# TensorE's order within a step of two attentions: value products ahead of the next pair's transposes

## The chip, the cores and the metric

The kernel is one program on one core of a Trainium2 chip. The metric is the time of one execution on the device in microseconds (us), of which the median of three runs is given. TensorE multiplies matrices, VectorE (DVE in the profile) and ScalarE (ACT) work on elements and may read TensorE's output banks, GpSimd (POOL) works on elements outside those banks, SyncE (SP) issues most transfers.

## The reference, cut to what matters

Two transformer layers and a third hybrid block are computed for 512 tokens and 16 meta tokens ahead of them. The change touches the attentions of the first two layers. Layer 0 has a differential attention of 4 heads (two softmaxes each, one subtracted from the other) and a dense attention of 8 heads over 2 key heads; layer 1 has 16 heads over 2 key heads that see a window of 128 tokens to each side, the meta tokens, and a sink.

```python
def _diff_attention(q, k, v, lam, table, pos):
...
        s = jnp.einsum('bqhcd,bshcd->bhcqs', qb, k).astype(jnp.float32) * scale + bias[None, :, None]
        p = jax.nn.softmax(s, axis=-1)
        attn = p[:, :, 0] - lam * p[:, :, 1]
        return jnp.einsum('bhqs,bshv->bqhv', attn.astype(v.dtype), v)
...
def _gqa_dense(q, k, v):
...
        s = jnp.einsum('bqkgd,bskd->bkgqs', qb, k).astype(jnp.float32) * scale
        p = jax.nn.softmax(s, axis=-1)
        return jnp.einsum('bkgqs,bskd->bqkgd', p.astype(v.dtype), v)
...
def _window_gqa(q, k, v, sinks, table):
...
        s = jnp.einsum('bqkgd,bskd->bkgqs', qb, kc).astype(jnp.float32) * scale + bias[None]
        s = jnp.where(visible, s, NEG_INF)
        sink_col = jnp.broadcast_to(sink[None, :, :, None, None], s.shape[:-1] + (1,))
        p = jax.nn.softmax(jnp.concatenate([s, sink_col], axis=-1), axis=-1)[..., :-1]
        return jnp.einsum('bkgqs,bskd->bqkgd', p.astype(vc.dtype), vc)
```

## The kernel before, in words

Every engine has its own instruction stream, written by hand, and the streams meet at semaphores. Most of the program is projections: TensorE multiplies weights, held as a high and a low part (`w_hi`, `w_lo`), with activations held likewise, three products for one (lines 1032 to 1034).

Between the projections lie two calls of `attend`: one for layer 0 (34 pairs, which the text calls A for the 17 of the differential attention and B for the 17 of the dense one), one for layer 1 (32 pairs, called C). A **pair** is a block of 128 queries with two heads (or two softmaxes). One pair takes four pieces of work on TensorE and three elsewhere:

- `scores(s)` (L1120): queries times keys of both heads into the banks `acc`. It waits for `s_stored`, by which DVE tells that it has taken the scores of the pair before.
- DVE's `tops(s)` (L2416) adds the bias, finds the row maximum and writes `probs`; ACT's `exponentials` (L1755) run once for each head; DVE's `shares(s)` (L2427 and L2430, or L2433 to L2435) and POOL (L923) divide by the sums. They tell `probs` and `scaled`.
- `turn(s)` (L1140 to L1148), four steps after its scores (`LAG = 4`): TensorE transposes the probabilities into the two banks `tps`, and the 16 meta columns into a bank of `ops_`. In part of the B pairs it also transposes one or two finished blocks of A that are carried along (L1148). It waits for `probs`, for `scaled`, for `p_stored` of the pair before (its `tps` banks must have been copied out), and for `o_stored` of its `ops_` bank, of which there are two that alternate.
- ACT's `copies(s)` (L1764, L1766, L1773) takes meta columns, carried blocks and the transposed probabilities out to `probsT`, and tells `p_stored`. In ACT's order it stands between the exponentials of head 0 and of head 1 of a later pair. It waits for `p_full`, which the last transpose of `turn(s)` tells.
- `values(s)` (L1162 in A, L1168 in B and C): transposed probabilities times values, into the same `ops_` bank. It waits for `p_stored` of this pair.
- DVE's `outputs(s)` (L2444 in A; L2449, L2451, L2453 in B and C) takes the result out and tells `o_stored`.

The steps are a loop over `s` on each engine. Step `s` on TensorE holds `turn(s - 4)`, `values(s - 5)` and `scores(s)`. In the first four steps pieces of a projection (`fill`) stand ahead of the scores. In the five steps behind the last scores, pieces of the next projection (`drain`, L960 to L962) take their place; the last two pieces in layer 0 wait for a result of `outputs`. `tps` has no second copy: its two banks are one for each head.

Of the kernel before, what the change touches and what calls it, by code (L numbers as in the profile page):

```python
# [53 lines left out]
LAG = 4  # L54
# [150 lines left out]
def transposed_blocks_program(nc, a, out):  # L205
# [80 lines left out]
    with ctx:  # L286
# [369 lines left out]
        for i in range(8):  # L656
            for t in range(4):
# [3 lines left out]
                n = (hi - lo) * P  # L661
# [274 lines left out]
        def _(pe):  # L936
# [9 lines left out]
            def close(ins, b, kind=""):  # L946
                ins.then_inc(sems[f"{kind}full{b}"], T.up(f"{kind}full{b}"))
                T.saw(f"{kind}stored{b}")
# [146 lines left out]
            def attend(pairs, metaT, fill, drain):  # L1095

                n = len(pairs)
# [3 lines left out]
                def scores(s):  # L1101
                    p = pairs[s]
                    if s and pairs[s - 1].differ and not p.differ:
                        T.saw("kswap_in", 5 * 16)
                        pe.wait_ge(sems["kswap_in"], T.at("kswap_in"))
                        T.saw("vmeta_in", 32)
                        pe.wait_ge(sems["vmeta_in"], T.at("vmeta_in"))
                    free = 2 * s if p.wide else 2 * s - 2
                    if s == 0:
                        for kind in ("stored0", "stored1"):  # L1110
                            pe.wait_ge(sems[kind], T.at(kind))
                    if free > 0:
                        pe.wait_ge(sems["s_stored"], stored_0 + free)
                    if p is A_METAS:
                        T.saw("q_metas", 2)
                        pe.wait_ge(sems["q_metas"], T.at("q_metas"))
                    left = [sum(x[0] == o for x in p.products) for o in range(2)]
                    for o, rows, c, w, q, keys, first, last in p.products:
                        bank = flat[o][:, LEAD:] if p.wide else acc[s % 2][:, o, :]
                        ins = mm(bank[rows, c:c + w], q, keys, start=first, stop=last)  # L1120
                        left[o] -= 1
                        if not left[o]:
                            ins.then_inc(sems[f"s_full{o}"], T.up(f"s_full{o}"))

                def turn(s):
                    p = pairs[s]
                    if s == 0:
                        for kind in ("t_stored0", "t_stored1"):
                            pe.wait_ge(sems[kind], T.at(kind))
                    pe.wait_ge(sems["probs"], probs_0 + s + 1)  # L1130
                    if not p.differ:
                        pe.wait_ge(sems["scaled"], scaled_0 + p.scaled)
                    if s:
                        pe.wait_ge(sems["p_stored"], copied_0 + s)
                    p.b = open_("o_")
                    unit = ident[0:p.nq, 0:p.nq]
                    _, which, to = p.turned_metas(ops_[p.b])
                    if p.joint:
                        both_heads = probs_1[0:p.nq, s % RING].rearrange("p o n -> p (o n)")
                        nc.tensor.transpose(to[:, 0, :], both_heads[:, SEQ:SEQ + 2 * N_META], unit)  # L1140
                    for o in (1,) if p.differ else (0, 1):
                        S = probs_1[0:p.nq, s % RING, o, :]
                        if not p.joint:
                            nc.tensor.transpose(to[:, o - which.start, :], S[:, p.meta:p.meta + N_META], unit)  # L1144
                        for k, c in enumerate(p.tiles[o]):
                            ins = nc.tensor.transpose(tps[o][:, k * P:k * P + p.nq], S[:, c:c + P], unit)  # L1146
                    for a, to in p.carried(ops_[p.b]):
                        ins = nc.tensor.transpose(to, a.dest, ident[:])  # L1148
                    ins.then_inc(sems["p_full"], T.up("p_full"))

                def values(s):
                    p = pairs[s]
                    pe.wait_ge(sems["p_stored"], copied_0 + s + 1)
                    b, last = p.b, len(p.tiles[0])

                    def weights(o, k):
                        return probsT_1[:, s % 2, o, k, :] if k < last else metaT[:, s % 2, 0 if p.joint else o, :]

                    if p.differ:
                        for k in range(last + 1):  # L1160
                            for rows, v in p.v:
                                ins = mm(ops_[b][rows, 0:v[k].shape[1]], weights(1, k)[:, rows], v[k],  # L1162
                                         start=k == 0, stop=k == last)
                    else:
                        for sums in (p.sums_of[n:n + 2] for n in range(0, len(p.sums_of), 2)):
                            for k in range(last + 1):
                                for o, rows, queries, to in sums:
                                    ins = mm(ops_[b][rows, to], p.v[o][k], weights(o, k)[:, queries],  # L1168
                                             start=k == 0, stop=k == last)
                    close(ins, b, "o_")  # L1170

                for s in range(n + LAG + 1):
                    if 0 <= s - LAG < n:
                        turn(s - LAG)
                    if 0 <= s - LAG - 1 < n:
                        values(s - LAG - 1)
                    if s < len(fill):
                        fill[s]()
                    if s < n:
                        scores(s)  # L1180
                    if s == n:
                        pe.wait_ge(sems["s_stored"], stored_0 + 2 * n)
                    if s >= n:
                        drain[s - n]()
# [128 lines left out]
            def value_tokens(qkv, v):  # L1313
# [10 lines left out]
                     [(1, k) for k in (0, 1, 2)]]  # L1324
            begun, drain = unit_ahead(MIX["even_out"], early, (3, 4))
            attend(A_PAIRS + B_PAIRS, metaT_e, unit_in_parts(LEN), drain)
            for kind in ("o_stored0", "o_stored1"):
                pe.wait_ge(sems[kind], T.at(kind))
# [14 lines left out]
            pe.wait_ge(sems["kswap_in"], T.at("kswap_in"))  # L1343
            begun, drain = unit_ahead(MIX["odd_out"], [[(0, k)] for k in range(LAG + 1)], ())
            attend(C_PAIRS, metaT_o, unit_in_parts(SEQ), drain)
            for kind in ("o_stored0", "o_stored1"):
                pe.wait_ge(sems[kind], T.at(kind))
# [2066 lines left out]
```

## Time and profile before

| | |
|---|---|
| median of 3 runs | 2178.78 us (2178.54 to 2185.92) |
| the profiled execution, first to last instruction | 2178.0 us; no other time of its own is shown |
| TensorE busy | 2152.0 us, 99% |
| VectorE, ScalarE, GpSimd busy | 1094.7, 817.1, 877.4 us |
| mean granted clock of TensorE | 0.996 |
| bytes moved | 210.69 MB |

The three runs lie within 0.34%, two of them within 0.01%. The profiled execution is 0.5 to 0.8 us shorter than the two fast ones, as its span leaves out what lies ahead of the first and behind the last instruction.

### The profile page before, as it was taken

The numbers are of one execution on the slowest core, as the hardware profiler recorded it, in microseconds if no ns is written. First come the engines' busy times: TensorE is split into PE (matmuls) and PEld (weight loads), VectorE is DVE, ScalarE is ACT, GpSimd is POOL, SyncE is SP. The second block draws the span as 40 slices with busy tenths as digits, with TensorE's granted clock in tenths as the row PEclk, the third lists the DMA queues.
The fourth block names the chain that finished last, engine by engine and source line by source line (L and its number), as shares of the span: only waits on it lengthen the run. The fifth ranks groups of instructions, "written<-read, shape, count | busy, mean of one in ns | idle before, by whom it ended". The sixth has DMA issues, their size and how long they took to land.

```text
span 2178.0 us, 32989 instructions
## 1 busy us (share of the span) xinstructions
PE 2152.0 (99%) x13003; PEld 1826.1 (84%) x13003; DVE 1094.7 (50%) x1677; ACT 817.1 (38%) x1358; POOL 877.4 (40%) x396
## 2 busy tenths in 40 slices
PE   8999999999999999999999999999999999999998
PEld 7987899999999767788888778888878788888886
DVE  5577655623633375430243379555664554443225
ACT  4248544213333374431243323243423432322224
POOL 2323534433443454444444433333434344444442
PEclk9999999999999999999999999999999999999999
DMA  5720145333433602333333375233223243332331
GB/s 161 173 57 2 37 129 157 88 88 117 127 96 91 188 2 59 88 96 97 88 95 97 87 166 168 64 92 87 79 80 94 78 117 95 96 94 84 96 102 61
DMA packets 375111, 210.69 MB, mean 97 GB/s; under 512 B 26464, under 2 KB 367553, under 8 KB 374097
## 3 DMA queue, kind: packets, MB, share of 16 engines
q1 hardware_dynamic: 364726, 192.60, 31.2%
q10 hardware_dynamic: 10266, 16.41, 2.8%
q8 instruction: 87, 1.43, 0.3%
q14 instruction: 32, 0.25, 0.0%
HBM read 196.96 MB, written 15.40 MB: 98 GB/s over the span
## 4 chain that ended last, share of the span: by engine, by line
issue 42%; PE 35%; POOL 19%; DVE 2%; ACT 1%; POOLq 0%; DVEq 0%; ACTq 0%
POOL w_lo L894 19%; PE acc L1032 8%; PE acc L1033 8%; PE acc L1034 8%; PE ops L1168 2%; PE acc L1120 2%; PE tps L1146 2%; PE ops L1162 1%; PE ops L1144 1%; PE acc L960 1%; PE tps L1092 0%; PE acc L962 0%; PE acc L961 0%; DVE probs L2416 0%; DVE a_n L2568 0%
## 5 line engine op out<-in xcount | busy, mean ns | idle before, releaser
L894 POOL TENSOR_TENSOR w_lo<-raw,w_hi 128x1024 fp32r<-128x1024 f32 x326 | 793.5, 2434 | 1165.7 <-ACT w_hi L1624 1155.9
L1624 ACT ACTIVATE w_hi<-raw 128x1024 fp32r<-128x1024 f32 x325 | 344.4, 1060 | 1028.8 <-PE acc L1034 1004.7
L1032 PE MATMUL acc<-hr_hi,w_hi 128*128 128x512 f32 x1056 | 421.8, 399 | 0.6 <-DVE qkv L3030 0.6
L1034 PE MATMUL acc<-hr_hi,w_lo 128*128 128x512 f32 x1056 | 417.8, 396 | 0.0
L1033 PE MATMUL acc<-hr_lo,w_hi 128*128 128x512 f32 x1056 | 417.6, 395 | 0.0
L1032 PE MATMUL acc<-hn_hi,w_hi 128*128 128x264 f32 (+1 forms) x872 | 256.9, 295 | 2.7 <-DVE hn_lo L2500 1.5
L1033 PE MATMUL acc<-hn_lo,w_hi 128*128 128x264 f32 (+1 forms) x872 | 253.4, 291 | 0.0
L1034 PE MATMUL acc<-hn_hi,w_lo 128*128 128x264 f32 (+1 forms) x872 | 253.2, 290 | 0.0
L1032 PEld LDWEIGHTS acc<-hr_hi,w_hi 128*128 128x128 f32 x1056 | 198.4, 188 | 49.4 <-issue 1.8
L1034 PEld LDWEIGHTS acc<-hr_hi,w_lo 128*128 128x128 f32 x1056 | 198.4, 188 | 48.0
L1033 PEld LDWEIGHTS acc<-hr_lo,w_hi 128*128 128x128 f32 x1056 | 198.5, 188 | 47.4 <-issue 0.7
L1032 PEld LDWEIGHTS acc<-hn_hi,w_hi 128*128 128x128 f32 x872 | 164.2, 188 | 7.1 <-DVE hn_lo L2500 1.4
L1033 PEld LDWEIGHTS acc<-hn_lo,w_hi 128*128 128x128 f32 x872 | 164.2, 188 | 2.6
L1034 PEld LDWEIGHTS acc<-hn_hi,w_lo 128*128 128x128 f32 x872 | 163.5, 188 | 2.4
L1032 PE MATMUL acc<-mid_hi,w_hi 128*128 128x264 f32 x512 | 146.7, 286 | 0.3 <-DVE hid L2879 0.3
L1033 PE MATMUL acc<-mid_lo,w_hi 128*128 128x264 f32 x512 | 146.1, 285 | 0.0
L1034 PE MATMUL acc<-mid_hi,w_lo 128*128 128x264 f32 x512 | 145.9, 285 | 0.0
L923 POOL TENSOR_SCALAR probs<-probs,stat 128x528 f32<-128x528 f32 (+2 forms) x49 | 73.6, 1502 | 108.2 <-DVE stat L2427 108.0
L1755 ACT ACTIVATE probs<-probs,stat 128x528 f32<-128x528 f32 (+2 forms) x132 | 85.8, 650 | 44.9 <-DVE stat L2416 44.9
L1032 PE MATMUL acc<-mr_hi,w_hi 128*128 128x512 f32 x256 | 101.3, 396 | 0.0
L1034 PE MATMUL acc<-mr_hi,w_lo 128*128 128x512 f32 x256 | 101.3, 396 | 0.0
L1033 PE MATMUL acc<-mr_lo,w_hi 128*128 128x512 f32 x256 | 101.3, 396 | 0.0
(467 smaller groups left out, 3788.3 us busy)
## 6 DMA issues: line engine op xcount, KB each, us to landing
raw<-in_w_up SPq DMA_DIRECT2D x64, 512.0 KB, 4.0
raw<-in_w_down SPq DMA_DIRECT2D x64, 512.0 KB, 3.7
raw<-in_w_in SPq DMA_DIRECT2D x56, 512.0 KB, 3.8
raw<-in_w_ffn_gate SPq DMA_DIRECT2D x22, 512.0 KB, 3.8
raw<-in_w_ffn_up SPq DMA_DIRECT2D x22, 512.0 KB, 3.8
raw<-in_w_in_even SPq DMA_DIRECT2D x18, 512.0 KB, 8.6
raw<-in_w_ffn_down SPq DMA_DIRECT2D x16, 512.0 KB, 3.7
raw<-in_w_in_odd SPq DMA_DIRECT2D x10, 512.0 KB, 5.6
```

The costliest lines, as they stand in the source:

```text
L894: nc.gpsimd.tensor_tensor(w_lo[:, part], raw[:, slot], w_hi[:, part].bitcast(F32), ALU.subtract).then_inc(sems["lo"], T.up("lo"))
L923: nc.gpsimd.tensor_scalar(S, S, st[:, 4:5], None, ALU.mult).then_inc(sems["scaled"], T.up("scaled"))
L960: mm(out, w_hi[:, part, k, :], x_hi, start=first, stop=False)
L1032: mm(out, w_hi[:, part, w0 + k, :], xh, start=s0, stop=False)
L1033: mm(out, w_hi[:, part, w0 + k, :], xl, start=False, stop=False)
L1034: ins = mm(out, w_lo[:, part, w0 + k, :], xh, start=False, stop=s1)
L1120: ins = mm(bank[rows, c:c + w], q, keys, start=first, stop=last)
L1144: nc.tensor.transpose(to[:, o - which.start, :], S[:, p.meta:p.meta + N_META], unit)
L1146: ins = nc.tensor.transpose(tps[o][:, k * P:k * P + p.nq], S[:, c:c + P], unit)
L1168: ins = mm(ops_[b][rows, to], p.v[o][k], weights(o, k)[:, queries], start=k == 0, stop=k == last)
L1624: fn(w_hi[:, n % 2], raw[:, n % 4], ACT.Copy).then_inc(sems["hi"], T.up("hi"))
L1755: fn(S, S, ACT.Exp, bias=st[:, o:o + 1], scale=-1.0, accum_out=p.den(st, o)).then_inc(sems["exp"], T.up("exp"))
```

## The change

The two calls in TensorE's step change places. Nothing else is changed: both wait for the same semaphores at the same values, and no other engine's stream differs.

```diff
                 for s in range(n + LAG + 1):
+                    if 0 <= s - LAG - 1 < n:
+                        values(s - LAG - 1)
                     if 0 <= s - LAG < n:
                         turn(s - LAG)
-                    if 0 <= s - LAG - 1 < n:
-                        values(s - LAG - 1)
                     if s < len(fill):
                         fill[s]()
                     if s < n:
                         scores(s)
```

TensorE in the attention of layer 1 before the change, from the scores of a pair with 273 keys on (`acc` holds scores, `tps` and `ops` receive transposes, `probsT` are the copied ones, `vtok` the values; in brackets the semaphores that an instruction waits for):

```order
L1120 MATMUL acc<-keys_o,qkv_o 128x273 [waits s_stored]
L1120 MATMUL acc<-keys_o,qkv_o 128x273
L1144 MATMUL ops<-ident,probs 16x128 [waits p_stored,o_stored0,scaled,probs]
L1146 MATMUL tps<-ident,probs 128x128 x3
L1144 MATMUL ops<-ident,probs 16x128
L1146 MATMUL tps<-ident,probs 128x128 x3
L1168 MATMUL ops<-probsT,vtok_o 64x128 [waits p_stored]
L1168 MATMUL ops<-probsT,vtok_o 64x128 x3
L1168 MATMUL ops<-metaT_o,vtok_o 64x128 x2
L1120 MATMUL acc<-keys_o,qkv_o 128x401 [waits s_stored]
```

The same place in the changed kernel:

```order
L1120 MATMUL acc<-keys_o,qkv_o 128x273 [waits s_stored]
L1120 MATMUL acc<-keys_o,qkv_o 128x273
L1168 MATMUL ops<-probsT,vtok_o 64x128 [waits p_stored]
L1168 MATMUL ops<-probsT,vtok_o 64x128 x3
L1168 MATMUL ops<-metaT_o,vtok_o 64x128 x2
L1144 MATMUL ops<-ident,probs 16x128 [waits p_stored,o_stored0,scaled,probs]
L1146 MATMUL tps<-ident,probs 128x128 x3
L1144 MATMUL ops<-ident,probs 16x128
L1146 MATMUL tps<-ident,probs 128x128 x3
L1120 MATMUL acc<-keys_o,qkv_o 128x401 [waits s_stored]
```

Between a pair's transposes (L1144, L1146) and its own value products (L1168), the value products of the pair before and the scores stood before; now the scores alone stand there.

ACT in the same attention, which is the same in both kernels:

```order
L1764 ACTIVATE metaT_o<-ops 16x256 [waits p_full]
L1773 ACTIVATE probsT<-tps 128x2x256
L1755 ACTIVATE probs,stat<-probs,stat 128x273 [waits s_stored] x2
L1764 ACTIVATE metaT_o<-ops 16x256 [waits p_full]
L1773 ACTIVATE probsT<-tps 128x2x384
```

The copies of one pair stand between the exponentials of two heads; nothing moved here.

TensorE behind the scores in layer 0, where pieces of the next projection (L960) stand in their place, as a difference:

```order
+L1168 MATMUL ops<-probsT,vtok_e 64x128 x8
+L1168 MATMUL ops<-metaT_e,vm_e 64x128 x2
 L1140 MATMUL ops<-ident,probs 32x128
 L1146 MATMUL tps<-ident,probs 128x128 x8
 L1148 MATMUL ops<-ident,qkv_e 128x128
-L1168 MATMUL ops<-probsT,vtok_e 64x128 x8
-L1168 MATMUL ops<-metaT_e,vm_e 64x128 x2
 L960 MATMUL acc<-mix_e_hi,w_hi 128x264
 L961 MATMUL acc<-mix_e_lo,w_hi 128x264
```

Here too the value products of the pair before have moved ahead of the transposes (L1140, L1146, L1148), and the projection's products follow these directly.

## Rows read from the trace of the kernel before

**Rows 1.** The page's first part: busy time, share of the span and instructions.
```profile
PE 2152.0 (99%) x13003; PEld 1826.1 (84%) x13003; DVE 1094.7 (50%) x1677; ACT 817.1 (38%) x1358; POOL 877.4 (40%) x396
```

**Rows 2.** Busy time, granted clock and transfers in A, B and C (stretches named in the text).
```profile
core 0: us, PE busy (x) PEld busy (x) DVE busy (x) ACT busy (x) POOL busy (x), PEclk, DMA share, GB/s
143.37:192.37 49.00, 48.30 (x405) 38.10 (x403) 41.68 (x129) 39.12 (x125) 3.04 (x2) 1.00 0.01 1
192.37:257.65 65.28, 61.38 (x674) 49.83 (x672) 42.27 (x138) 49.49 (x119) 38.25 (x34) 1.00 0.01 2
755.47:837.90 82.43, 80.48 (x774) 54.62 (x774) 57.94 (x231) 62.69 (x177) 38.91 (x30) 1.00 0.01 1
```

**Rows 3.** Timeline, TensorE in C: start us, us, what, [idle before <-releaser].
```profile
786.41 0.73 PE L1120 MATMUL acc<-keys_o,qkv_o 64*128 64x273 f32 x4
787.29 0.27 PE L1144 MATMUL ops<-ident,probs 128*16 128x128 f32 x1 [0.15 <-DVE mix_o_lo L2453]
789.06 0.94 PE L1120 MATMUL acc<-keys_o,qkv_o 64*128 64x401 f32 x4
...
789.94 0.27 PE L1144 MATMUL ops<-ident,probs 128*16 128x128 f32 x1
```

**Rows 4.** Timeline, DVE in C: the last instruction of an output.
```profile
786.85 0.29 DVE L2453 TENSOR_TENSOR mix_o_lo<-ops,mix_o_hi 128x128 fp32r<-128x128 f32 x1
```

**Rows 5.** Timeline, end of C: value products begin, ACT copies the transposes just finished.
```profile
833.72 0.78 ACT L1773 ACTIVATE probsT<-tps 128x768 f32<-128x768 f32 x1
...
835.98 0.88 PE L1168 MATMUL ops<-probsT,vtok_o 128*64 128x128 f32 x12
836.09 0.37 ACT L1764 ACTIVATE metaT_o<-ops 16x256 f32<-16x256 f32 x1 [1.59 <-PE tps L1146]
836.37 0.57 ACT L1773 ACTIVATE probsT<-tps 128x512 f32<-128x512 f32 x1
```

**Rows 6.** Timeline, B: two copies of ACT around its table loads, TensorE's next transposes.
```profile
204.36 1.00 ACT L1773 ACTIVATE probsT<-tps 128x1024 f32<-128x1024 f32 x1
...
209.90 1.00 ACT L1773 ACTIVATE probsT<-tps 128x1024 f32<-128x1024 f32 x1
...
211.15 0.27 PE L1140 MATMUL ops<-ident,probs 128*32 128x128 f32 x1 [1.73 <-ACT probsT L1773]
```

**Rows 7.** Timeline, TensorE in a step of B with nothing carried.
```profile
199.09 0.28 PE L1140 MATMUL ops<-ident,probs 128*32 128x128 f32 x1
...
201.42 0.49 PE L1120 MATMUL acc<-qkv_e 64*128 64x264 f32 x1
...
202.51 0.29 PE L1140 MATMUL ops<-ident,probs 128*32 128x128 f32 x1
```

**Rows 8.** Timeline, B with two carried blocks: TensorE, ACT's copies, the end of the output.
```profile
228.02 1.09 PE L1168 MATMUL ops<-probsT,vtok_e 128*64 128x128 f32 x16
...
228.12 0.27 ACT L1764 ACTIVATE metaT_e<-ops 32x128 f32<-32x128 f32 x1 [0.58 <-PE ops L1148]
...
228.80 1.00 ACT L1773 ACTIVATE probsT<-tps 128x1024 f32<-128x1024 f32 x1
...
229.26 1.16 PE L1120 MATMUL acc<-kx_e,qkv_e 64*128 64x264 f32 x8
...
230.23 0.28 DVE L2453 TENSOR_TENSOR mix_e_lo<-ops,mix_e_hi 128x128 fp32r<-128x128 f32 x1
...
230.66 0.27 PE L1140 MATMUL ops<-ident,probs 128*32 128x128 f32 x1 [0.24 <-DVE mix_e_lo L2453]
```

**Rows 9.** Timeline, end of B: a piece of the projection, the next transposes.
```profile
245.04 0.39 PE L960 MATMUL acc<-mix_e_hi,w_hi 128*128 128x264 f32 x1
...
246.24 0.27 PE L1140 MATMUL ops<-ident,probs 128*32 128x128 f32 x1
```

**Rows 10.** Timeline, A: ACT's copies of a pair.
```profile
156.72 0.25 ACT L1764 ACTIVATE metaT_e<-ops 16x128 f32<-16x128 f32 x1
156.87 0.57 ACT L1773 ACTIVATE probsT<-tps 128x512 f32<-128x512 f32 x1
```

**Rows 11.** The one stretch of 5 us with a low granted clock (columns as rows 2).
```profile
460.00:465.00 5.00, 5.00 (x54) 5.00 (x52) 0.04 (x1) 0.00 (x0) 0.00 (x0) 0.52 0.36 108
```

## The prediction

> **What bounds the kernel now.** I read the page first, then the busy time by stretches, then the timeline of the attentions. The page says that TensorE is busy 99% of the span [rows 1], so each microsecond that it waits more ends up in the time, unless something later takes it back. By stretches [rows 2] the attentions are where it waits: A is 49.0 us with 0.7 idle, B 65.3 with 3.9, C 82.4 with 1.95. The clock is full in all three, and DMA stands still (share 0.01), so the change can act only through TensorE's own order and its partners ACT and DVE. The timeline then tells for whom it waits. In C the transposes that follow the scores of 273 keys start at 787.29, though these scores end at 787.14; DVE's output ended at 786.85 + 0.29 = 787.14 as well, and its word takes 0.15 us more [rows 3, 4]. In B with two carried blocks the output ends at 230.51, and the transposes start at 230.66 after 0.24 idle [rows 8]. So today a turn waits for the output of the pair two before it, which has only the scores' time to be taken out. That is what the change relieves: with the value products first, the output has the time of a whole turn more.
>
> **What the change takes instead.** Call the times of the pieces V (values), T (turn), S (scores). ACT's copies of a pair must come between its T and its V. Before, V of the pair before and S lay in between; now S alone does. The copies need a time L from the end of T to the start of V:
>
> - ACT starts 0.10 to 0.11 after the next piece of TensorE has begun (835.98 to 836.09 [rows 5], 228.02 to 228.12 [rows 8]).
> - The meta columns hold it 0.28 in C (836.09 to 836.37 [rows 5]), 0.15 in A [rows 10]; for B I take 0.17, between the two. In B two carried blocks lengthen 228.12 to 228.80 = 0.68 [rows 8], so each carried block is (0.68 - 0.17) / 2 = 0.25.
> - The large copy is 0.57 for two key tiles and 0.78 for three in C [rows 5], 1.00 in B [rows 6, 8], 0.57 in A [rows 10].
> - From the end of ACT's copy to TensorE's start: 209.90 + 1.00 = 210.90 to 211.15, that is 0.25, of which 0.03 is the weight load that goes ahead, so 0.22 [rows 6]. The nearest other row, DVE to TensorE, has 0.15 [rows 4].
>
> So L is 0.11 + 0.28 + 0.57 + 0.22 = 1.18 in C with two tiles and 1.39 with three; in B 0.11 + 0.17 + 1.00 + 0.22 = 1.50, 1.75 and 2.00 with 0, 1 and 2 carried blocks; in A 0.11 + 0.15 + 0.57 + 0.22 = 1.05.
>
> The cover S is, start to start, 1.09 in A and B (201.42 to 202.51 [rows 7]), 0.88 in C with 401 keys (789.06 to 789.94 [rows 3]), and for 273 keys 0.73 - 0.06 = 0.67, since the record of 401 is 0.94 for the 0.88. Tiles and keys go together, as the scores four pairs on are those of the same query block. Where the scores are over, a piece of the projection covers: 1.20 in B [rows 9]; in C I take 0.88, its three products of 512 columns being near to the scores of 401 keys.
>
> ACT is free when T ends. The exponential that stands ahead of the copies comes behind DVE's read of one head's scores, and I estimate both done 1.5 us after these end; V and T lie between, 1.77 us in C (787.29 to 789.06 [rows 3]) and 3.42 - 1.09 = 2.33 in B [rows 7]. Behind the waiting V stand T and S on TensorE's queue, and for S waits DVE. Both then move as one, and no other queue holds anything of this. The SP and POOL queues are not passed by anything.
>
> **The sum, C.** Each of 27 turns that scores follow waits L - S = 1.18 - 0.67 or 1.39 - 0.88, that is 0.51 both times: 13.8 us. The four last ones wait 0.30, 0.51, 0.51, 0.30: 1.6. Turn 0 waits for its copies before and after alike. What goes is today's waiting: 1.95 us idle [rows 2], and in 13 steps another 0.07 which the record's tail hides (787.29 - 786.41 - 0.67 = 0.21 in place of the 0.15 shown): 2.9. **C: 15.4 - 2.9 = +12.5 us.**
>
> **B.** Five turns with nothing carried wait 1.50 - 1.09 = 0.41: 2.05. One meets ACT's table loads: its copies end 5.54 us after those before it (204.36 to 209.90 [rows 6]) where a step is 3.42 (199.09 to 202.51 [rows 7]): 2.12, in place of today's 1.73. One with one carried block waits 0.66. Four with two wait 0.91 each, 3.64; a fifth is followed by the meta queries' scores, 12 products for 4 on half the rows, which I estimate at twice 1.09, so it waits for nothing. The turn of the meta queries copies its meta columns as C does and one block: 0.77. Four at the end wait 0.80, 0.53, 0.53 and, where only 3 of 9 products are left for cover (0.40), 1.35. Sum 12.4. What goes: 3.9 idle [rows 2] and 7 times 0.07: 4.4. **B: +8.0 us.**
>
> **A.** L = 1.05 against S = 1.09: nothing waits, but with 0.04 us to spare. The idle 0.7 us [rows 2] goes. **A: -0.7 us.**
>
> Nothing takes this back later: behind both attentions TensorE runs projections whose weights ACT and POOL prepare after the copies, and the prepared unit has about 0.3 us to spare by my count. The sum is 12.5 + 8.0 - 0.7 = **+19.8 us on the profiled 2178.0: 2197.8**. The median of the runs is 0.8 above the profiled span, so the forecast is **2198.5 us** (+0.9%).
>
> **Bounds.** The least sure term is ACT's word to TensorE, paid in 47 waits. By DVE's 0.15 instead of 0.22 to 0.25 it is 3.3 to 4.7 us less. From above, 0.1 us more each time, for a start of TensorE out of a stop, makes 4.7 us more, and 17 times 0.1 in A, whose spare is thin, 1.7: 2194 to 2205.
>
> **The rivals.**
>
> *The output wait is the dearer one (not slower).* The two orders trade one wait for another. If ACT's copies came back within 0.67, 0.88 and 1.09 us, all waits for outputs would go, 0.7 in A, 4.4 - 1.73 = 2.7 in B and 2.9 in C, 6.3 us in all: 2172.5. It decides at L = S. The rows put L of C 0.51 above it with both parts recorded, so I give it 0.04, of which 0.01 for a gain above 0.5%.
>
> *Half is hidden.* If TensorE's waits in a step also let DVE and ACT get ahead, so that every second copy comes early, about 10 us remain: 2188.8. Against it: the copies hang on the end of T by `p_full`, and cannot begin before it. 0.05.
>
> *ACT becomes the bound.* Copies that wait longer push the second head's exponentials and all behind them. ACT is 80% used in A and 76% in B and C [rows 2]. If each of 66 steps took 0.3 us more on top, it would be 2218. In steps longer than today's there is more room for ACT, not less. 0.02.
>
> *The clock.* In the one stretch with a low clock TensorE shows no idle time at all; it runs the small products of `kernel_products` there, and has fallen to about 0.52, near the lower level of 1.2 GHz [rows 11]. So waiting is not the only thing that lowers it, and the 1.73 us of idle time in B left the clock of its stretch at 1.00 [rows 2, 6]. If it fell to 1.2 GHz for all of C, C's 80.5 us of work would double: 2279. 0.02. The Trainium skill (TensorE: Matmul & The Clock Gate, section "A second HAM failure mode: psum-queue depth-cycling") speaks against this change: short idle times between groups of products, as each step cycles through the banks, can make the clock swing between its levels. By it C and perhaps B would go this way; here no row shows it so far, as waits of 0.15 to 0.24 us in many steps left the clock full.
>
> *The change doesn't do what it says* is ruled out by the order of the instructions: every step is turned round, and only on TensorE.
>
> **How the numbers follow.** The forecast has 0.87. 0.5% is 10.9 us, about what a measurement of this kernel can tell from no change. Slower by more: 0.87 + 0.02 + 0.02 = 0.91; within: 0.03 + 0.05 = 0.08; faster: 0.01. The range takes the bounds 2194 to 2205, goes down to 2190 for part of the hidden case, and up to 2206 for the scatter of runs: 2190 to 2206.
>
> **What would show it.** In the profile after, the first value product of nearly every step (L1168) has idle time ahead of it released by ACT's L1773, some 0.4 to 0.5 us in C, 0.3 to 0.9 in B, and in A (L1162) none or hundredths. The transposes (L1140, L1144) no longer wait for DVE. Four steps of C take 4 x 0.51 - 2 x 0.21 = 1.6 us more than today, C's stretch is 95 us long and B's 73. The rest of the program keeps its length. I am wrong if the waits at L1168 are there but the stretches don't grow, if A's value products wait 0.2 us or more, or if the clock of a stretch falls.

## The result, and the profile after

The changed kernel takes **2193.97 us** (median of 5 runs, 2193.05 to 2194.66). The kernel before, run beside it, takes 2180.6 (5 runs, 2178.54 to 2185.92). The ratio is 1.0057, interval 1.0041 to 1.0073: slower by 0.6%. The forecast was 2198.5 in 2190 to 2206, so direction and range held, and the size was 4.5 us too large. The profiled execution has a span of 2192.7 us against 2178.0, which is 14.7 us more where the sum said 19.8.

The page's first part after, to be held against [rows 1]:

```profile
PE 2155.4 (98%) x13003; PEld 1827.5 (83%) x13003; DVE 1090.9 (50%) x1677; ACT 819.6 (37%) x1358; POOL 876.5 (40%) x396
```

The same stretches of A, B and C as in [rows 2], each from the like instruction to the like instruction, with the same columns:

```profile
143.30:192.42 49.12, 49.12 (x404) 38.35 (x402) 41.59 (x129) 40.68 (x125) 3.12 (x2) 1.00 0.00 1
192.42:263.04 70.62, 61.54 (x674) 49.57 (x672) 41.36 (x138) 48.92 (x119) 37.95 (x33) 1.00 0.01 2
762.34:852.37 90.03, 81.14 (x774) 54.17 (x774) 55.42 (x232) 62.68 (x177) 39.16 (x30) 1.00 0.01 1
```

A is 49.12 us long (before 49.00), B 70.62 (65.28), C 90.03 (82.43). TensorE's busy time grows by only 0.8, 0.2 and 0.7 us in them; B now has 9.1 us idle and C 8.9. The clock is full in all three, as it was. What TensorE waits for is one thing (waits of TensorE in C, then in B; columns: who waits and for whom, us in total, times, longest):

```profile
PE ops L1168 <- ACT probsT L1773: 9.2, 32, 0.5
```

```profile
PE ops L1168 <- ACT probsT L1773: 9.1, 16, 2.0
```

The value products of all 32 pairs of C and of 16 of the 17 of B wait for ACT's copy, and in B and C no row of the transposes names DVE any more: the wait of [rows 3] and of [rows 8] is gone. Now two steps of C on TensorE:

```profile
790.48 0.94 PE L1120 MATMUL acc<-keys_o,qkv_o 64*128 64x401 f32 x4
791.70 0.88 PE L1168 MATMUL ops<-probsT,vtok_o 128*64 128x128 f32 x12 [0.28 <-ACT probsT L1773]
...
793.48 0.73 PE L1120 MATMUL acc<-keys_o,qkv_o 64*128 64x273 f32 x4
794.49 0.33 PE L1168 MATMUL ops<-probsT,vtok_o 128*64 128x128 f32 x2 [0.28 <-ACT probsT L1773]
```

and ACT in the same two:

```profile
790.59 0.37 ACT L1764 ACTIVATE metaT_o<-ops 16x256 f32<-16x256 f32 x1 [0.90 <-PE tps L1146]
790.87 0.78 ACT L1773 ACTIVATE probsT<-tps 128x768 f32<-128x768 f32 x1
...
793.59 0.37 ACT L1764 ACTIVATE metaT_o<-ops 16x256 f32<-16x256 f32 x1 [0.68 <-PE tps L1146]
793.87 0.57 ACT L1773 ACTIVATE probsT<-tps 128x512 f32<-128x512 f32 x1
```

The terms of the forecast stand here one behind the other. ACT starts 0.11 after the scores have begun, spends 0.28 until the large copy begins, and 0.78 or 0.57 on it: all four are as forecast. But the copy ends at 791.65, and the value products start at 791.70. **ACT's word, the time from the end of its copy to TensorE's start, takes 0.05 us, not 0.22.** So the lag is 1.22 and 1.01 against covers of 0.88 and 0.67, and a step waits 0.34, where 0.51 stood in the sum. (The record shows 0.28, since the scores' record has a tail of 0.06.) It is 0.05 in B as well, at the shortest wait (202.32 + 1.00 = 203.32, and the products at 203.37) and at the longest, 2.05 us, where ACT loads its tables (its copy ends at 212.52):

```profile
202.32 1.00 ACT L1773 ACTIVATE probsT<-tps 128x1024 f32<-128x1024 f32 x1
```

```profile
203.37 1.09 PE L1168 MATMUL ops<-probsT,vtok_e 128*64 128x128 f32 x16 [0.17 <-ACT probsT L1773]
...
212.57 1.09 PE L1168 MATMUL ops<-probsT,vtok_e 128*64 128x128 f32 x16 [2.05 <-ACT probsT L1773]
```

### The profile page after: what moved, and what is told of

It is laid out like the page before. It is cut to its first block, busy times and chain, and to the rows that moved or that the text cites. A ratio compares the mean times of both kernels' runs of the same rounds, so it can differ in the third digit from the quotient of the medians.

```text
span 2192.7 us, 32989 instructions
## 1 busy us (share of the span) xinstructions
PE 2155.4 (98%) x13003; PEld 1827.5 (83%) x13003; DVE 1090.9 (50%) x1677; ACT 819.6 (37%) x1358; POOL 876.5 (40%) x396
## 3 DMA queue, kind: packets, MB, share of 16 engines
q1 hardware_dynamic: 364726, 192.60, 31.1%
## 4 chain that ended last, share of the span: by engine, by line
issue 42%; PE 35%; POOL 19%; ACT 3%; DVE 2%; POOLq 0%; DVEq 0%; ACTq 0%
POOL w_lo L894 19%; PE acc L1032 8%; PE acc L1033 8%; PE acc L1034 8%; PE ops L1168 2%; PE tps L1146 2%; ACT probsT L1773 2%; PE acc L1120 1%; PE ops L1162 1%; PE ops L1144 1%; ACT metaT_o L1764 1%; PE tps L1092 0%; PE acc L960 0%; PE acc L962 0%; PE acc L961 0%
## 5 line engine op out<-in xcount | busy, mean ns | idle before, releaser
L1032 PEld LDWEIGHTS acc<-mid_hi,w_hi 128*128 128x128 f32 x512 | 97.4, 190 | 0.5 <-DVE hid L2879 0.5
```

Source lines behind the costliest of these rows:

```text
L1032: mm(out, w_hi[:, part, w0 + k, :], xh, start=s0, stop=False)
```

## The experiments

A trace is easiest to compare in five stretches of TensorE. "Lead" goes to the first scores of layer 0. "A+B" goes from there to the end of that attention's last value product, and "C" is the like in layer 1. "Between" lies between the two attentions, and "rest" behind C. One profile of each kernel, us:

| kernel | lead | A+B | between | C | rest | span |
|---|---|---|---|---|---|---|
| before | 131.06 | 127.90 | 486.46 | 93.36 | 1339.22 | 2178.0 |
| after | 130.99 | 133.36 | 488.14 | 100.76 | 1339.45 | 2192.7 |
| e1 new order in C alone | 129.49 | 127.90 | 486.30 | 100.76 | 1343.25 | 2187.7 |
| e2 new order in A and B alone | 130.85 | 134.76 | 486.36 | 93.33 | 1346.70 | 2192.0 |
| e3 bank wait late | 130.98 | 126.53 | 484.67 | 91.79 | 1340.13 | 2174.1 |
| e4 two copies | 130.22 | 129.41 | 486.62 | 92.49 | 1342.06 | 2180.8 |
| e5 copy wait last | 130.80 | 128.33 | 486.42 | 96.49 | 1346.76 | 2188.8 |
| e6 three more waits | 131.34 | 133.39 | 486.38 | 100.78 | 1339.01 | 2190.9 |
| e7 values last | 129.39 | 159.02 | 488.23 | 114.12 | 1339.44 | 2230.2 |
| e8 before, rot_s first | 131.09 | 127.92 | 486.26 | 93.36 | 1339.67 | 2178.3 |
| e9 after, rot_s first | 129.25 | 133.37 | 485.23 | 100.75 | 1340.90 | 2189.5 |
| e10 bank wait late, rot_s first | 131.42 | 126.55 | 488.58 | 91.76 | 1340.49 | 2178.8 |
| e11 copy wait last, rot_s first | 131.02 | 128.30 | 486.25 | 96.53 | 1340.10 | 2182.2 |
| e12 one more wait | 131.30 | 133.39 | 486.39 | 100.78 | 1342.84 | 2194.7 |

Kernels with like code in an attention agree there to 0.05 us, except where the clock fell (e2, e4, below). The change itself is therefore 5.46 + 7.40 = **12.9 us**. The other 1.8 of the 14.7 lie in stretches that the change does not touch, and those differ by up to 7.8 us ("rest" in e5 and e6) between kernels with the same code there.

**e1 and e2: one attention at a time.** The step's order hangs on a condition, which in e2 is turned round (e1 against the changed kernel):

```diff
+                    first = not pairs[0].wide
-                    if 0 <= s - LAG - 1 < n:
+                    if first and 0 <= s - LAG - 1 < n:
                         values(s - LAG - 1)
                     if 0 <= s - LAG < n:
                         turn(s - LAG)
+                    if not first and 0 <= s - LAG - 1 < n:
+                        values(s - LAG - 1)
```

> New order in the attention of layer 1 alone, old order in layer 0. The theory (the copies' lag L against the scores' time S, step by step) says that each attention pays for itself: C was 7.4 us longer in the changed kernel, so the span is 2178.0 + 7.4 = 2185.4 us, with waits for ACT's copies (L1773) only in C, 0.34 us a step. The second theory, that 1.8 us of the loss came from the small products of kernel_products falling differently against the clock, says that these take 9.2 us here as before, since they come ahead of C. The rival, that the loss hangs on something shared by both attentions or carried from one to the other, has no reason for 7.4.

> New order in layer 0 alone. The theory: A unchanged within 0.2 us, B +5.3, C as before. With the clock's part, the small products begin 5.4 us later as in the changed kernel and take 10.9 us instead of 9.2: span 2185.1. If the clock's part is chance from run to run and not set by where the products begin, the span is 2183.3 or anything up to 2 us around it. With the run of layer 1 alone the two gains should add up to the 14.7 us of the whole change.

Measured: e1 2187.82 us (8 runs, 2185.44 to 2194.61), ratio 1.0034, interval 1.0021 to 1.0048. e2 2191.52 (7 runs, 2181.64 to 2193.95), ratio 1.0037, interval 1.0022 to 1.0052. The kernel before had 2179.9 beside them (30 runs, 2176.51 to 2187.36). The stretches give what was expected: e1 carries all of C and nothing of A and B, e2 the reverse and 1.4 us more. Against the median of the kernel before, e1 is 7.9 us slower (7.4 expected) and e2 11.6 (5.3 to 7.1 expected); the interval of e2's ratio, 4.8 to 11.3 us, is wide enough to hold what was expected. The profiled execution of e2, 14.0 us longer than that of the kernel before, shows two places for the excess. The first is behind ACT's table loads in B, where TensorE's wait of 2.05 us was followed in this run by a lower clock (windows of e2, columns as [rows 2]):

```profile
205.00:210.00 5.00, 4.83 (x51) 3.75 (x49) 3.61 (x13) 4.29 (x7) 1.62 (x1) 1.00 0.02 3
210.00:215.00 5.00, 2.95 (x31) 2.40 (x28) 2.63 (x9) 3.80 (x9) 0.90 (x2) 0.88 0.00 0
215.00:220.00 5.00, 5.00 (x44) 3.68 (x42) 2.24 (x8) 2.72 (x6) 5.00 (x6) 0.78 0.00 2
```

The same place with the same wait kept the full clock in after, e6, e9 and e12, and fell to 0.66 in e4. The fall costs e2 134.76 - 133.36 = 1.4 us. The second place, in "rest", is met again in e5.

**e3: the output wait without the new order.** The gain that the change was after, in the old order. A turn first transposes into `tps`, which needs no `ops_` bank, and waits for the bank only ahead of the meta columns:

```diff
-                    p.b = open_("o_")
                     unit = ident[0:p.nq, 0:p.nq]
+                    heads = (1,) if p.differ else (0, 1)
+                    for o in heads:
+                        for k, c in enumerate(p.tiles[o]):
+                            nc.tensor.transpose(tps[o][:, k * P:k * P + p.nq], probs_1[0:p.nq, s % RING, o, c:c + P], unit)
+                    p.b = open_("o_")
...
```

> Old order of the steps; inside a turn the probabilities are transposed first and only then does TensorE wait for the output bank (o_stored), ahead of the meta columns. The theory says that the old order waits for outputs only as these have the scores' time alone; they get 0.44 to 0.87 us more, so these waits vanish: 2.9 us in C, about 1.7 in B (the wait of the next projection at its end stays), up to 0.7 in A: 4.6 to 5.3 us less, span about 2173, give or take 1.8 for the clock of the small products. If TensorE's waits there were not for the bank but the cost of going from one kind of product to another, nothing changes, or it becomes slower by the extra waits.

Measured: span 2174.1; A+B is 1.4 and C 1.6 us shorter, 2.9 together where 4.6 to 5.3 were expected. TensorE's idle time did fall by 1.8 us in A+B and 2.1 in C, but its busy time grew by 0.5 in each, which the expectation had at nothing. TensorE and DVE in C of e3:

```profile
780.35 0.73 PE L1120 MATMUL acc<-keys_o,qkv_o 64*128 64x273 f32 x4
...
780.80 0.29 DVE L2454 TENSOR_TENSOR mix_o_lo<-ops,mix_o_hi 128x128 fp32r<-128x128 f32 x1
781.02 0.65 PE L1139 MATMUL tps<-ident,probs 128*128 128x128 f32 x4
```

The turn starts 0.67 behind the scores and 0.07 before DVE's output has ended: the cover of 0.67 for 273 keys, which the forecast had only estimated, is right. The median did not show the gain: 2181.98 (12 runs, 2176.07 to 2189.5), ratio 1.0009, interval 0.9998 to 1.002. They scatter over 13 us; e8 to e10 deal with that.

**e4: shorter copies in the new order.** TensorE tells ACT by a new semaphore `p_half` when the transposes of head 0 are done, and ACT copies these while head 1 is transposed:

```diff
+                        if o == 0:
+                            ins.then_inc(sems["p_half"], T.up("p_half"))
...
+                    if not p.differ:
+                        act.wait_ge(sems["p_half"], half_0 + 1 + sum(not x.differ for x in pairs[:s]))
+                        fn(probsT_1[:, s % 2, 0, 0:k, 0:p.nq].rearrange("p k q -> p (k q)"),
+                           both[:, 0, 0:k * P], ACT.Copy).then_inc(sems["metas"], T.up("metas"))
                     act.wait_ge(sems["p_full"], full_0 + s + 1)
```

> Changed kernel, but ACT copies head 0's transposes as soon as they are done, then the meta columns and head 1. L falls to 0.80 and 0.90 us in C (waits 0.13 and 0.02 a step instead of 0.34), in B to 0.90, 1.15 and 1.40 (waits 0, 0.06, 0.31 instead of 0.24, 0.49, 0.74). The theory: C 8.3 us shorter and B 5.1, so the span goes from 2192.7 to 2179.3, give or take 1.8. The rival, that ACT is the bound in the new order, says that two copies in place of one (0.15 us more of ACT in each step) make it slower: 2192.7 + 49 x 0.15 = 2200.

Measured: 2181.25 us (10 runs, 2177.1 to 2188.19), ratio 1.0009, interval 0.9995 to 1.0022. C is 92.49, 8.3 us less than after, as expected: the wait was the copies' length, and with half of it ahead of the turn's end it is nearly gone (0.3 us left at L1170 in C). A+B is 129.41, 4.0 less than after where 5.1 was expected, in a run whose clock was 0.66 from 210 to 215 us. The rival of ACT as the bound, which had the span at 2200, falls.

**e5: which wait stands last.** In a turn of the old order, the wait for `p_stored` is put behind the one for `o_stored`:

```diff
-                    if s:
-                        pe.wait_ge(sems["p_stored"], copied_0 + s)
                     p.b = open_("o_")
+                    if s:
+                        pe.wait_ge(sems["p_stored"], copied_0 + s)
```

> Old order; in a turn the wait for ACT's copies (p_stored) stands behind the wait for the output bank instead of ahead of it, with the same values. My sum had 0.22 to 0.25 us from the end of ACT's copy to TensorE's transposes, measured where another wait stood behind it; in the changed kernel the value products, with this as their only wait, start 0.05 us after the copy. If a wait that stands behind the released one costs time, the one place in B where transposes wait for ACT (the table loads) shows less than 0.25 us here, about 0.15, and the waits for DVE's outputs 0.05 to 0.1 us more than 0.15. If it is the kind of instruction and not the number of waits, 0.25 stays. The time stays within 1.5 us of the kernel before either way.

Measured: one run of 2190.74, 11.2 us above the kernel before beside it (2179.59), where 1.5 at most was expected. Part of it is in C, 3.1 us longer. DVE, then TensorE in C of e5:

```profile
779.77 0.29 DVE L2453 TENSOR_TENSOR mix_o_lo<-ops,mix_o_hi 128x128 fp32r<-128x128 f32 x1
...
780.32 0.27 PE L1144 MATMUL ops<-ident,probs 128*16 128x128 f32 x1
```

The output ends at 780.06 and the turn starts 0.26 later, where it was 0.15 in [rows 3, 4]. And behind ACT's table loads, where this turn waits for `p_stored`, the copy ends at 209.32 + 1.00 = 210.32 and the turn starts 0.14 later instead of 0.25:

```profile
209.32 1.00 ACT L1773 ACTIVATE probsT<-tps 128x1024 f32<-128x1024 f32 x1
...
210.46 0.27 PE L1140 MATMUL ops<-ident,probs 128*32 128x128 f32 x1 [1.47 <-ACT probsT L1773]
```

The two words have changed places. The trace shows why, as it also holds the wait instructions of TensorE's queue (PEldq; no busy time, starts in tenths of a us). A turn of B or C has more waits than its first weight load carries. Before, one instruction waits for `p_stored` (L1134), the next for `o_stored` and `scaled` (L943), and the load itself for `probs`; at the table loads of [rows 6], where the copy ends at 210.90 and the transposes start at 211.15:

```profile
L1134 PEldq EVENT_SEMAPHORE  x1: 51/51/51, 210.9 to 210.9; - x1
```

```profile
L943 PEldq EVENT_SEMAPHORE  x1: 51/51/51, 211.0 to 211.0; - x1
```

In e5 `p_stored` stands in the second of the two, with `scaled`, and only the load is behind it; the transposes start at 210.46:

```profile
L1135 PEldq EVENT_SEMAPHORE  x1: 51/51/51, 210.4 to 210.4; - x1
```

So in a turn, what is waited for in the last wait instruction arrives 0.14 to 0.15 after its sender's record ends, and what stands in the one before it 0.25 to 0.26. One wait instruction more costs 0.11 us, and 27 turns of C with 0.11 more would make 3.0 of the 3.1. The forecast read ACT's word off a wait with another wait instruction behind it [rows 6].

The other 7.5 us are in "rest", about 1291 us. DVE and TensorE there:

```profile
1293.73 2.73 DVE L3041 TENSOR_TENSOR qkv<-qkv,rot_s 32x1024 f32<-32x1024 f32 x1 [8.99 <-DMA rot_s<-rot_t]
```

```profile
1297.11 1.11 PE L1092 MATMUL tps<-ident,qkv 128*128 128x128 f32 x4 [5.31 <-DVE qkv L3030]
```

In the kernel before this DVE instruction waited 4.57 us, and the transposes of TensorE behind it did not wait at all. In e5 two transfers `rot_s` landed late (10.6 and 9.7 us after their issue, before 6.9 and 7.0), and TensorE stood for 5.31 us; then the clock fell (windows):

```profile
1291.00:1296.00 5.00, 0.81 (x4) 0.32 (x2) 2.27 (x1) 1.06 (x1) 2.34 (x1) 1.00 1.28 170
1296.00:1301.00 5.00, 3.89 (x12) 3.02 (x12) 3.06 (x9) 2.32 (x5) 0.00 (x0) 0.51 0.42 117
```

TensorE's idle time here was none in before, after, e6 and e7, 0.35 us in e3, 2.4 to 2.9 in e12, e1 and e4, and 5.3 in e2 and e5. "Rest" is 2.8 to 4.0 us longer in the middle group, and 7.5 in the last. None of these kernels differ there in a single instruction.

**e6 and e12: more waits at the value products.** In the source three waits more on `probs`, already met, stand behind the wait for `p_stored` in `values` (e6), or one (e12):

```diff
                     pe.wait_ge(sems["p_stored"], copied_0 + s + 1)
+                    for _ in range(3):
+                        pe.wait_ge(sems["probs"], probs_0 + s + 1)
```

> Changed kernel with three more waits behind p_stored ahead of the value products, all for something that has long come (probs of the same pair). If each wait behind the released one costs 0.06 to 0.1 us, the value products start 0.23 to 0.35 us after the end of ACT's copy instead of 0.05, and 47 waits make it 8 to 14 us slower, 2201 to 2207; A, whose copies come just in time, adds up to 3. If waits cost nothing once they are satisfied, 0.05 stays and the span is that of the changed kernel.

> The changed kernel with one more wait, already met, on the semaphore probs behind the wait for p_stored in the value products. ACT's word reaches the value products 0.05 us after its copy ends, and the transposes of the kernel before 0.25 us after it, with the wait for o_stored behind p_stored; with p_stored as the last wait it was 0.14. Theory 'a wait behind it costs 0.11': here the value products start 0.16 behind the copy, the attention of layer 1 is 31 x 0.11 = 3.4 us longer than the 100.8 of the changed kernel and that of layer 0 16 x 0.11 = 1.8 longer than 133.4. Rival 'it hangs on the instruction that waits, not on the count of waits': 0.05 and both lengths as in the changed kernel, as with three such waits.

Measured: one run each, 2192.8 and 2196.69 us; A+B and C as in after to 0.03 us, and in e12 the rest is longer at the late transfer. The program has 66 instructions more in e12 and 132 in e6, so the waits are there. The value products still start 0.05 us behind the copy. ACT and TensorE in C of e12, and the added wait of the same step:

```profile
789.47 0.78 ACT L1774 ACTIVATE probsT<-tps 128x768 f32<-128x768 f32 x1
...
790.30 0.33 PE L1169 MATMUL ops<-probsT,vtok_o 128*64 128x128 f32 x2 [0.28 <-ACT probsT L1774]
```

```profile
L1154 PEldq EVENT_SEMAPHORE  x1: 51/51/51, 787.6 to 787.6; - x1
```

**But these two runs don't test what they were made for.** In the program as it ran, the added wait is over at 787.6, 2.7 us ahead of the value products: it stands ahead of the wait for `p_stored`, not behind it, and that wait is carried by the weight load of the first value product itself. So it is for all 66 pairs of both runs, by 0.9 us at the least. They show that 66 and 132 wait instructions met long before cost nothing, and say nothing of one that stands behind.

What they leave open, whether the word hangs on the kind of product or on the wait instructions behind the released wait, the kernel before decides with one and the same kind of product, the projection's first. Here one wait instruction (L1025, at 15.1) stands between DVE's word and the product:

```profile
14.26 0.76 DVE L2500 SCALAR_TENSOR_TENSOR hn_lo<-h,gains,hn_hi 128x528 fp32r<-128x528 f32 x1
...
15.16 0.36 PE L1032 MATMUL acc<-hn_hi,w_hi 128*128 128x264 f32 x1 [0.77 <-DVE hn_lo L2500]
```

Here the weight load carries the wait, and no wait instruction stands there:

```profile
17.22 0.76 DVE L2500 SCALAR_TENSOR_TENSOR hn_lo<-h,gains,hn_hi 128x528 fp32r<-128x528 f32 x1
...
18.04 0.39 PE L1032 MATMUL acc<-hn_hi,w_hi 128*128 128x264 f32 x1 [0.26 <-DVE hn_lo L2500]
```

The first starts 15.16 - 15.02 = 0.14 behind DVE's end, the second 18.04 - 17.98 = 0.06. So the kind of product doesn't matter. The word takes 0.05 to 0.06 with no wait instruction behind the released wait, 0.14 to 0.15 with one and 0.25 to 0.26 with two. For the value products themselves no run shows the step, as none puts a wait instruction there.

**e7: the third order.** Turn, scores, values. The copies have scores and value products as cover, and the outputs nothing, as the turn that takes their bank follows them (against the kernel before):

```diff
                     if 0 <= s - LAG < n:
                         turn(s - LAG)
-                    if 0 <= s - LAG - 1 < n:
-                        values(s - LAG - 1)
                     if s < len(fill):
                         fill[s]()
                     if s < n:
                         scores(s)
+                    if 0 <= s - LAG - 1 < n:
+                        values(s - LAG - 1)
```

> Third order: transposes, scores, then the value products, so that nothing covers DVE's output before the next turn, while the copies keep scores and values as cover. The theory of lags says that each turn waits for the whole output: in C 0.11 + 0.61 + 0.15 = 0.87 us, 27 us in all; in B 0.83 and 0.26 more for each carried block, some 18; in A 0.28 + 0.26 = 0.54, 9; less the 7 of today's waits: +47 us, span 2225. So the output's wait would be the dearer one, and the changed order the middle one of three. If the output bank was never what bound it, the span stays near 2178.

Measured: one run of 2232.09 us; A+B 31.1 longer and C 20.8. The forecast of +47 was 5 us short, and that close only by luck: C came out about 3 below its part (27 less the 2.9 of before), A+B some 8 above. There the scores wait as well, which no term held. The waits in A+B, then in C:

```profile
PE acc L1120 <- DVE stat L2416: 8.3, 17, 0.8
```

```profile
PE ops L1144 <- DVE mix_o_lo L2453: 21.9, 27, 0.8
```

The outputs' way, bare of its cover, costs 0.8 us in each of 27 steps, more than twice the 0.34 of the copies'. So the three orders rank: cheapest where the shorter way, the outputs', has the scores as its cover (old), next where the longer one, the copies', has them alone (new), dearest where a way has no cover (e7).

**e8 to e11: the place of the late transfer.** In layer 2 ACT issues three transfers `u_chunk` and behind them two `rot_s`. Here they change places:

```diff
-                    if n == 0:
+                    if n == 0 and x != 1:
                         fetch_u(3 * x, min(3 * x + 3, CHUNK))
...
                     if x == 1:
                         rotate(n)
+                    if n == 0 and x == 1:
+                        fetch_u(3, 6)
```

> The kernel before, with one thing else: in layer 2, where the runs so far differ, ACT issues the two transfers rot_s ahead of the three u_chunk instead of behind them. Theory 'late transfer': of the traces so far four (new order in layer 1 only, in layer 0 only, two copies, copy wait last) have TensorE idle for 2.7 to 5.3 us ahead of L1092 because DVE waited for rot_s, and the clock falls behind it; in all it takes 2.8 to 7.9 us and scatters the runs of every kernel. Then here the runs lie within 5 us of each other, no idle time over 1 us ahead of L1092 at that place, and the median is 2177 to 2180. Rival 'the place is only where a scatter from elsewhere shows': the runs still spread over 10 us and a stall of some us is seen there or behind it in one of the four kernels of this call.

> The changed kernel with the same exchange of the two issues. The stages say +0.1 in A, +5.3 in B, +7.4 in C and 0 to 1.8 at the small products (clock): 12.9 to 14.6 above the run with the old order and the same exchange, if nothing else in the program hangs on the order. If the part at the small products belongs to the change, it is 14.6; if it is the clock's phase, it is anything from -1.8 to +1.8 on 12.9.

> The old order with the transposes into tps ahead of the wait for the ops_ bank, and the exchange of the two issues. By the lengths of A, B and C in its first profile (1.4 and 1.6 us shorter) it is 3.0 us faster than the old order with the exchange, plus or minus 1.8 for the clock at the small products. If instead the gain was luck of one profile, it is 0.

> The old order with p_stored waited for last in a turn, and the exchange. First run: 0.4 us more in A and B, 3.1 in C (every turn starts 0.26 behind DVE's output in place of 0.15), and 7.9 at the late transfer. Theory 'late transfer': now 3.5 us above the old order with the exchange (within 1.8). Rival: the 7.9 belong to this edit, and it is 11 above again.

Measured, with the kernel before at 2179.88 (30 runs, 2177.75 to 2188.78):

| | median us | runs | ratio to before, interval |
|---|---|---|---|
| e8 before, rot_s first | 2179.53 | 12, 2177.28 to 2184.11 | 0.9993, 0.9981 to 1.0005 |
| e9 after, rot_s first | 2192.85 | 7, 2189.37 to 2196.44 | 1.0049, 1.0032 to 1.0066 |
| e10 bank wait late, rot_s first | 2179.15 | 12, 2174.53 to 2180.86 | 0.9986, 0.9974 to 0.9997 |
| e11 copy wait last, rot_s first | 2183.5 | 10, 2182.14 to 2187.09 | 1.001, 0.9997 to 1.0023 |

In all four profiles the wait ahead of L1092 is gone; what comes in its place is a short wait for `u_chunk` (0.67 us in e8, 1.97 in e9). e5's 7.5 us went with it: e11 is 4.0 above e8, of which 0.4 and 3.2 stand in A+B and C. So the late transfer made most of that run's surprise, not the edit. The runs spread over 5.0 to 7.1 us where those of e1 to e4 did over 9 to 13, and those of the kernel before over 11.0 here; the 5 expected for e8 came out as 6.8. And e9 is 13.3 us above e8, where the two attentions say 12.9: the change's price, seen without the other place. e10 is the one version whose interval lies below 1, by 0.14% of the kernel before, but it holds two edits; against e8, which holds one of them, its median shows 0.4 us of the 3.0 that its attentions are shorter. Its one profile lost 2.3 of them "between".

That stretch is what remains. It holds the small products of `kernel_products`, the only place with a low clock in [rows 11]. The granted clock there, first before, then after:

```profile
465.00:470.00 5.00, 5.00 (x27) 4.96 (x27) 0.76 (x2) 0.00 (x0) 0.00 (x0) 0.50 0.00 0
470.00:475.00 5.00, 5.00 (x42) 5.00 (x41) 0.00 (x0) 0.97 (x1) 0.00 (x0) 0.95 0.00 0
```

```profile
465.00:470.00 5.00, 5.00 (x51) 5.00 (x50) 0.48 (x1) 0.00 (x0) 0.00 (x0) 0.50 0.37 105
470.00:475.00 5.00, 5.00 (x37) 4.96 (x38) 0.76 (x2) 0.00 (x0) 0.00 (x0) 0.50 0.01 3
```

The 64 products of L1273 took 371 ns at the median after, and 259 ns before:

```profile
L1273 PE MATMUL ops<-ct,pw_re x64: 259/371/371, 461.3 to 472.2; 64*128 64x16 f32 x64
```

```profile
L1273 PE MATMUL ops<-ct,pw_re x64: 259/259/371, 455.8 to 465.0; 64*128 64x16 f32 x64
```

At the full clock one takes 259 ns, at a granted clock of 0.50 it takes 371, and how many of the 64 fall on either side differs from trace to trace: "between" is 486.2 to 486.6 in nine traces, 488.1 to 488.6 in three (after, e7, e10) and 484.7 and 485.2 in e3 and e9. Old and new orders stand in every group, so it is not the change that decides it; what does was not tried.

## Why the prediction was right, and where it was off

**What bounds the kernel, and the sign: right.** The output waits went, and the copies' wait took their place, in B and C at each step. The rival in which the output's was the dearer wait falls: it had 6.3 us for it, and in e3 the old order gains 2.9 in all when the wait goes.

**The lag's parts.** 0.11, 0.28 or 0.17, 0.57, 0.78 and 1.00 came out to 0.01 us, and a carried block costs 0.25: with two, the value products start at 224.63, 1.83 behind the scores, for 2.00 forecast less the 0.17 of the word. The covers of 0.67, 0.88 and 1.09 hold too (e3).

**The mis-sized term is "from the end of ACT's copy to TensorE's start", 0.22.** It measured 0.05. The forecast took it from a turn's wait [rows 6], where two wait instructions stand between the word and the first load, and applied it to value products, whose first load carries their only wait. e5 takes one of the two away and shows it to be worth 0.11; the two projection products of the kernel before put the last one at 0.08. The term's lower bound, DVE's 0.15, was again a turn's, with one wait instruction in it, so the 3.3 to 4.7 us allowed for it were too little. Over 47 waits 0.17 makes 8.0 us: C 12.5 - 31 x 0.17 = 7.2 (measured 7.4 by the length of the attention, 7.6 by the stretch), B 8.0 - 16 x 0.17 = 5.3 (measured 5.3).

**A: no loss, as said, but no gain either.** The wait ahead of the turn went, and the step is no shorter. TensorE in A before, and after:

```profile
155.14 0.27 PE L1144 MATMUL ops<-ident,probs 128*16 128x128 f32 x1
...
155.69 1.06 PE L1162 MATMUL ops<-vtok_e,probsT 128*128 128x128 f32 x8
...
156.90 1.16 PE L1120 MATMUL acc<-qkv_e 64*128 64x264 f32 x8
...
158.06 0.27 PE L1144 MATMUL ops<-ident,probs 128*16 128x128 f32 x1
```

```profile
155.09 1.16 PE L1162 MATMUL ops<-vtok_e,probsT 128*128 128x128 f32 x8
...
156.31 0.27 PE L1144 MATMUL ops<-ident,probs 128*16 128x128 f32 x1
...
156.95 1.16 PE L1120 MATMUL acc<-qkv_e 64*128 64x264 f32 x8
...
158.04 0.49 PE L1162 MATMUL ops<-vtok_e,probsT 128*128 128x128 f32 x2
```

From the turn to what follows it takes 0.55 before and 0.64 after; from the scores on, 1.16 before and 1.09 after. Over A the two sums change by +1.4 and -1.4 us, and the value products add 0.1. The forecast counted pieces as if each had one length wherever it stands. Here scores behind a turn cost 0.09 more than value products behind a turn, and no row names a releaser for it. That is another 0.8 of the error, with the opposite sign.

**The rest.** "Keeps its length" was wrong by 1.8 us, though not through the change: the small products took 1.7 longer, the stretch behind C 0.2. That this went against the largest error is luck. With the terms put right the sum is 19.8 - 8.0 + 0.8 + 1.8 = 14.4, for 14.7 measured. The 0.8 from profiled span to median was read off different executions: the profiled one after took 2194.66 us for its span of 2192.7, 2.0 more, and was the slowest of the five, so that the median lies 1.3 above the span.

**The clock.** In after it stayed full in A, B and C, with a wait in each step of B and C. The Trainium skill (TensorE: Matmul & The Clock Gate, section "A second HAM failure mode: psum-queue depth-cycling") speaks of idle times between groups of products that let the clock swing. Waits of 0.2 to 0.7 us in 47 steps did not do so in after, e6, e9 and e12, nor did those of C alone in e1; in C of e7 TensorE was idle for 22.5 of 114.1 us, at a clock of 1.00. A single wait of 1.95 to 2.05 us was followed by a lower clock in two of the six that have it (e2, e4), and cost 1.4 us in e2. Why in these two and not in the others stays open.

## What to carry to other kernels

When an order of work trades one wait for another, write down for each partner its way there and back and what covers it in either order; here the copies' way of 1.0 to 1.8 us took the place of the outputs' shorter one under the same cover, and that settled the sign before any run. Read the price of a semaphore's word where as many wait instructions stand between the released wait and the work as will stand there after the change, and look in the trace where a wait really stands, not in the source. And compare traces by stretches: two attentions that repeat to 0.05 us gave 12.9 us for the change, where the unchanged code beside them moved by up to 7.8 in single profiles.

## What the runs showed of the hardware

- The word of one and the same ACT instruction took 0.05 us to value products, whose weight load carries the wait (48 times in after), 0.14 to a turn's transposes with one wait instruction ahead of their load (e5), and 0.25 with two (before). 66 and 132 more wait instructions, met 0.9 us or more ahead, cost nothing measurable (e12, e6).
- Two transfers of 64 KB that landed 7.0 us after their issue in the kernel before took 10.1 in e5, where the issue of the first had itself taken 2.3 us instead of 0.6. That moved a run by 7.5 us, of which 5.3 was idle TensorE and the rest TensorE at the lower of its two clocks behind it.
- TensorE without idle time fell to a granted clock of 0.50 in products of 16 columns, in each trace, but not from the same product on.
